# Two transformer blocks on one core: bursts of constant products in TensorE's waits, and ScalarE's untaken path written as loops

## The reference

```
first block, per layer l:
  mod = silu(c) @ w_ada[l] + b_ada[l]            # shifts, scales, gains
  h = norm(x) * (1 + sc1) + sh1
  mix = attention(h)                             # global GQA + three dilated groups, gates
  x = norm(a * x + g1 * mix);  h = norm(x) * (1 + sc2) + sh2
  scores = sigmoid(h @ w_router)                 # 16 experts in 4 groups
  best group, then 2 experts of it; y = sum of silu(h @ gate) * (h @ up) @ down
  x = norm(a * x + g2 * y)
second block: layer 0 gated linear attention, layer 1 differential attention with a relative bias,
  each with an MoE of 16 experts (hidden width 512, in the first block 256), 2 of a group chosen
```

## Time and profile before

| | us |
|---|---|
| median of 3 runs | 1534.39 (1533.79 to 1534.82) |
| the profiled execution's own time | 1536.67 |
| its span, first to last instruction | 1534.9 |
| mean granted TensorE clock | 0.970 |
| busy: PE / DVE / ACT / POOL | 1426.8 (93%) / 546.7 (36%) / 329.3 (21%) / 147.6 (10%) |
| chain that ended last | PE 83%, DMA 7%, DVE 5%, ACT 2%, issue 1% |
| HBM read | 458.24 MB, 301 GB/s over the span |

### The profile page before, as it was taken

One profiled execution on the slowest core, in us unless ns is written; L12 is line 12 of the kernel. 1 busy time (PEld: TensorE's weight loads), 2 busy tenths in 40 slices (PEclk: granted clock), 3 DMA queues, 4 the chain that ended last, 5 costly groups with the idle time before them and its releaser, 6 DMA issues.

```text
span 1534.9 us, 15763 instructions
## 1 busy us (share of the span) xinstructions
PE 1426.8 (93%) x6564; PEld 810.7 (53%) x6564; DVE 546.7 (36%) x1065; ACT 329.3 (21%) x716; POOL 147.6 (10%) x103
## 2 busy tenths in 40 slices
PE   6999999799799999889989998999988998999995
PEld 3686885344378788444336444444435764444432
DVE  2591245532575124553251233121114353322113
ACT  3112231321210323131123132111112343111101
POOL 1007820000002920000000000000000000000000
PEclk8999999899999999989999999999998999999998
DMA  9996352899657741389946557899999408799995
GB/s 376 412 374 241 143 220 110 329 428 418 277 237 287 271 165 56 140 359 429 418 186 244 195 237 311 340 427 429 426 428 400 165 1 338 288 428 427 428 429 236
DMA packets 36873, 462.52 MB, mean 301 GB/s; under 512 B 4120, under 2 KB 6440, under 8 KB 8216
## 3 DMA queue, kind: packets, MB, share of 16 engines
q1 hardware_dynamic: 34112, 448.91, 71.2%
q0 software_dynamic: 1648, 10.39, 1.7%
q10 hardware_dynamic: 1032, 2.10, 0.7%
HBM read 458.24 MB, written 3.15 MB: 301 GB/s over the span
## 4 chain that ended last, share of the span: by engine, by line
PE 83%; DMA 7%; DVE 5%; ACT 2%; issue 1%; SPq 0%; DVEq 0%
PE work L684 12%; PE work L1072 12%; PE acc L684 7%; PE work L667 7%; DMA ring<-in_stream 7%; PE work L957 7%; PE work L1118 6%; PE acc L667 5%; PE work L972 3%; PE acc L817 3%; PE work L676 3%; PE work L1026 2%; PE work L1538 2%; PE acc L1683 2%; PE work L883 2%
## 5 line engine op out<-in xcount | busy, mean ns | idle before, releaser
L684 PE MATMUL work<-ht_sb,ring 128*128 128x256 f32 x576 | 128.0, 383 | 2.1 <-DMA ring<-in_stream 1.6
L684 PEld LDWEIGHTS work<-ht_sb,ring 128*128 128x128 f32 x576 | 110.2, 192 | 19.9 <-DMA ring<-in_stream 2.4
L684 PE MATMUL acc<-ht_sb,ring 128*128 128x256 f32 x512 | 114.0, 381 | 0.0
L1072 PE MATMUL work<-ring,area 128*64 128x512 f32 x480 | 107.9, 593 | 3.4 <-DMA ring<-in_stream 3.4
L684 PEld LDWEIGHTS acc<-ht_sb,ring 128*128 128x128 f32 x512 | 96.1, 190 | 14.8 <-issue 2.0
L667 PE MATMUL work<-ring,ht_sb 128*128 128x512 f32 (+1 forms) x224 | 92.6, 573 | 5.1 <-DMA ring<-in_stream 2.9
L1840 ACT ACTIVATE area<-work 128x512 f32<-128x512 f32 (+1 forms) x53 | 30.6, 590 | 238.8 <-PE work L684 120.7
L2910 DVE SCALAR_TENSOR_TENSOR area<-area,comb_slot,work 128x512 f32<-128x512 f32 x16 | 12.0, 748 | 190.8 <-ACT area L2037 190.8
L535 POOL DMA_DIRECT2D ln_sb<-in_ln_vecs x8 | 4.4, 556 | 778.2 <-DMA early<-in_stream 443.9
L817 PE MATMUL acc<-area_r,mt_sb_r 128*128 128x512 f32 x256 | 71.7, 409 | 5.2 <-DVE area_r L2818 4.3
L667 PE MATMUL acc<-ring,mt_sb 128*128 128x512 f32 x160 | 71.4, 595 | 2.6 <-DVE mt_sb L3138 2.6
(11 more groups left out here) (394 smaller groups left out, 2081.6 us busy)
## 6 DMA issues: line engine op xcount, KB each, us to landing
ring<-in_stream SPq DMA_DIRECT2D x136, 2048.0 KB, 14.8
area<-in_stream SPq DMA_DIRECT2D x46, 2048.0 KB, 15.5
cst<-in_stream SPq DMA_DIRECT2D x14, 2048.0 KB, 14.9
early<-in_stream SPq DMA_DIRECT2D x14, 2048.0 KB, 21.4
ln_sb<-in_ln_vecs POOLq DMA_DIRECT2D x8, 1024.0 KB, 12.2
rel_rows<-mt_sb ACTq DMA_DIRECT2D x1, 2048.0 KB
area<-in_stream SPq DMA_DIRECT2D x2, 1024.0 KB, 10.0
mt_sb<-in_stream SPq DMA_DIRECT2D x2, 1024.0 KB, 16.2
```

What stands on the lines that cost most here:

```text
L684: ins = pe.matmul(dst, w[:, k, c0:c0 + n], src[:, k0 + k, :], start=k == 0, stop=k == ks - 1)
L1072: ins = pe.matmul(banks[half][e * CAP:(e + 1) * CAP, :], tokens[:, k, at:at + CAP], w[:, e, half * W:(half + 1) * W], start=k == 0, stop=k ...
```

## The change

TensorE gets `stay_warm(n)`: n products of a tile of ones with one column of it, spread to 512 columns, in bf16, into a bank that is free there; nobody reads them. Bursts of it are put ahead of and between waits; some of these waits are new and ask for something earlier than the wait that was there. ScalarE's general path becomes three nested loops with two steps written out, so that a loop body has 18 transfers (`moe`).

```diff
+            def stay_warm(n, bank=work[0]):
+                for _ in range(n):
+                    pe.matmul(bank[:, :], ones_h[:, :], ones_h[:, 0:1].to_broadcast([P, W]), start=True, stop=True)
...
             def route_logits(n, ready, between=None):
+                stay_warm(2 if between is None else 5)
                 flip_rows(1, 1, ready)
+                stay_warm(3)
                 route_part(1)
                 fold_part(n, 1)
                 if between is not None:
                     between()
 
+            def await_choice(number):
+                if number < DEPTH:
+                    stay_warm(4)
+                    pe.wait_ge(tokens_scaled, TT * (number + 1))
+                    stay_warm(3)
+                    pe.wait_ge(scores_made, number + 1)
+                    stay_warm(9)
+                    pe.wait_ge(x_hi_ready, TT * (number + 1))
+                    stay_warm(2)
+                else:
+                    stay_warm(2)
+                    pe.wait_ge(logits_made, number + 1)
+                    stay_warm(10)
+                pe.wait_ge(chosen_ready, C.seen(chosen_ready))
+                pe.wait_ge(tables_loaded, 16 * 3)
...
-            def counts():
-                pe.wait_ge(chosen_ready, C.seen(chosen_ready))
-                pe.wait_ge(tables_loaded, 16 * 3)
-                pe.wait_ge(consts_set, 3)
+            def counts(number):
+                await_choice(number)
...
                 pe.matmul(work[1][:, 0:NE], ones_h[:, :], CHOSEN[:, 1, :], start=False, stop=True).then_inc(counted, 1)
+                stay_warm(4)
...
             ada_finish(*ADA_FIRST[3], parts_3)
+            pe.wait_ge(consts_set, 3)
+            stay_warm(4)
+            for k in range(2):
+                pe.wait_ge(ht_by_act, k + 1)
+                stay_warm(3)
             for l in range(DEPTH):
                 if l:
                     spread_silu()
+                    stay_warm(4)
+                    pe.wait_ge(silu_row_ready, 4)
+                    stay_warm(10)
+                    pe.wait_ge(var_ready, 9)
+                    stay_warm(3)
                     flip_tokens(0)
+                    stay_warm(3)
                     await_tokens()
                     wait_acc_free()
-                    pe.wait_ge(silu_row_ready, 4)
...
                       start=True, stop=True).then_inc(filled, 1)
+            stay_warm(3, work[1])
+            pe.wait_ge(var_ready, 17)
+            stay_warm(5, work[1])
             flip_tokens(0)
...
             moe(2, F_2 // P)
+            stay_warm(6)
+            pe.wait_ge(var_ready, 23)
+            stay_warm(5)
             flip_tokens(0)
...
-                with act.Fori(0, PAIRS) as i:
-                    for step in range(steps):
-                        e, f = step // fc, step % fc
-                        act.wait_ge(rest["steps_done"], i * steps + (TT + PAIRS + step))
+                with act.Fori(0, PAIRS) as i, act.Fori(0, 2) as e, act.Fori(0, fc // 2) as d:
+                    for h in range(2):
+                        act.wait_ge(rest["steps_done"], i * steps + e * fc + d * 2 + (TT + PAIRS + h))
                         for q in range(fc):
...
-                                act.dma_start(dst[:, q * ks:(q + 1) * ks, :], w[:, :, o:o + P]).then_inc(rest["loaded"], 16)
+                                act.dma_start(dst[:, q * ks:(q + 1) * ks, :], w[:, :, bass.ds(o, P)]).then_inc(rest["loaded"], 16)
```

More of the change, by code:

```diff
@@ L863, in moe_narrow @@
                 s0, before_pairs = SLOTS[MOE_NAMES[number]], PAIRS * number
-                counts()
+                counts(number)
                 pe.wait_ge(late_drained, len(ADA_LATE) * (number + 1))
@@ L2010, in all_tokens @@
                             for half, dst in enumerate((ALL_GATE, ALL_UP)):
-                                o = (2 * e + half) * fc * P + f * P
-                                act.dma_start(dst[:, q * ks:(q + 1) * ks, :], w[:, :, o:o + P]).then_inc(rest["loaded"], 16)
[L2013 to L2016, removed]
+                                o = e * (2 * fc * P) + d * (2 * P) + (half * fc + h) * P
+                                act.dma_start(dst[:, q * ks:(q + 1) * ks, :], w[:, :, bass.ds(o, P)]).then_inc(rest["loaded"], 16)
+                        w = stream[bass.ds(i * per_pair + d + (s0 + fc), 1), :, :].rearrange("a p n -> p (a n)")
+                        act.dma_start(ALL_DOWN, w[:, bass.ds(e * D + h * 2 * D, D)]).then_inc(rest["loaded"], 16)
+                        act.wait_ge(rest["summed"], i * steps + e * fc + d * 2 + (h + 1))
                         act.activation(ALL_SILU, work[0][:, 0:T], ACT.Silu).then_inc(rest["silu"], 1)
```

## The result

The changed kernel takes 1521.25 us, median of 5 runs (1520.36 to 1521.64), the kernel before 1534.82 (1533.79 to 1536.89, 5 runs): ratio 0.9904, 95% interval 0.9893 to 0.9915. That is 13.6 us won by the medians and 14.7 by the ratio (13.0 to 16.4 by its interval), where 15.3 were forecast (1519.1; the median lies 2.1 above, inside the range).

The account below looks back on a forecast made before the run. TensorE was taken to bound the kernel, with seven stretches at the lower clock behind its waits. Terms of 16.2 us less 0.9 for overruns and gaps gave 15.3, so 1534.4 - 15.3 = 1519.1 us; range 1513 to 1529 (8 in 10).

Parts of the forecast that it names:

- The bound: Whole kernel: TensorE sets the pace (chain 83% PE, 7% DMA), so time won on it is carried to the end.
- bound by DMA: Rival, 5%: the MoEs wait for weight transfers anyway, so their 7.1 us of gain vanish: 1526.2 us.
- First block's gathers: Behind the choice of experts in the first block's two MoEs: a warm clock halves cold gathers, worth 2.29 and 2.84 us.
- The product's price: One burst product of 512 columns: 0.22 us warm, 0.44 cold, taken from a gather's; bounds 0.1 and 0.44.
- Second block's gathers: Behind the choice in the second block's two MoEs: 1.0 us each of 1.7, limited by low parts and ScalarE's copies.
- Norms: Projections behind three layer norms (418.81, 792.74, 1160.57): no longer cold, worth 1.45, 2.23 and 2.64 us.
- ScalarE's delay: Norm behind the third MoE: looping the jumped-over path removes the table load's delay, 2.8 us; rival that it stays, 10%.
- The rule on transposes: Within a 16% rival: flips don't engage the high clock, so projections at 792.74 and 1160.57 lose 4.9 us: 1524.0.
- First loads: Products behind the first modulation rows: worth 0, since time won only lengthens the wait for a weight block at 68.78.
- The eight terms: Four for gathers, three for norms, one for ScalarE: 2.29 + 2.84 + 1.0 + 1.0 + 1.45 + 2.23 + 2.64 + 2.8 = 16.2 us.
- the second fall of the clock in the first layer: Behind the weight-block wait at 68.78: left as it is, with no gain counted for it.

Follow-up runs that it names:

- part 6: Changed kernel with ScalarE's inner loop over d written out, so 36 transfers stand in the wide path instead of 18: 1527.6 us, one run.
- part 5: Changed kernel without the ten products behind the first loads (1520.71 us), or with bursts at two more waits (1519.23, 1520.68); its table counts clock falls in fourteen traces.

## Why the prediction was right, and where not

- **The bound.** Right: the lead grew where TensorE's clock or ScalarE's wait changed, and it was carried to the end through every MoE. The doubled bursts show the same for lost time. Of the rival "bound by DMA" nothing was seen.
- **First block's gathers.** 2.29 + 2.84 forecast, 2.1 + 2.7 in the traces. The bursts fit as reckoned: the choice comes no later (10.36 us behind the flips in the trace after, 10.35 before). The product's price, 0.22 taken from the gathers for want of a row, is what the doubled burst measures.
- **Second block's gathers.** 1.0 each forecast, 0.8 and 0.9 measured. The low parts and ScalarE's copies do hold part of it back.
- **Norms.** 1.45, 2.23 and 2.64 forecast; 1.45, 2.2 and 2.6. The wait of the projections for VectorE's x_sb grew from 0.53 to 1.39 us behind faster flips, as said.
- **ScalarE's delay.** 2.8 forecast; 2.9 in the trace, 3.2 (1.8 to 4.8 by the interval) with the loops alone. That 18 transfers would be short enough was right; that length alone decides isn't borne out (part 6).
- **The rule on transposes** (the Trainium skill, TensorE: Matmul & The Clock Gate, Part 4: PE-mode transpose), by which 1524.0 would have come: not seen in the changed kernel. Between 1145.21 and 1147.70 only flips run, and the projection behind them starts at 1.00, as do the two at 414.36 and 785.72. With the halved bursts the clock holds across the flips behind the third MoE, but falls right behind those of the second block's norm (flips at 786.41, 0.51 from 789 on), so in that kernel the rule isn't excluded.
- **First loads.** Worth nothing, as the run without them shows, but the reason given was wrong. The wait for the weight block became shorter (1.60 to 1.04 us) where it was to become longer, and the burst overran the value it waits for by over 1 us, more than the 0.3 that the prediction allowed. It cost nothing because the warm projection made up for it.
- **Where it missed.** By little, and not clear of noise: 15.3 were forecast, and the ratio's interval reaches from 13.0 to 16.4. The eight terms measure 15.6 us together in the traces (forecast 16.2), where the medians leave 13.6. The step that doesn't hold is the one behind the sum, that the rest of the kernel is alike in both. The prediction left the second fall of the clock in the first layer "as it is", and took from one profile of before which places are cold. Behind waits of 1 to 2 us (68, 150 and 521 us) the clock falls in some executions and not in others. In the two profiled executions this gave 1.7 and took 1.6. By the table of part 5 it takes more from the changed kernel than from the one before: 9 of 12 against 1 of 12, at 1.7 us each in two places, is an estimated 2.3 us, about what the medians lack. That these falls are the missing 2 us is argued, not shown, since the executions behind the medians have no trace.

## What to carry to other kernels

Look for stretches in which TensorE is busy at the lower clock behind a wait of its own, fill the wait with wide products of constants into a free bank up to the moment the awaited value comes, and count one such product as long as a real one of the same columns (0.22 us): an overrun of the wait is passed on to the end like a gain. Fill the wait nearly to its end and take away other engines' delays in it first, since with 2.9 us left empty behind the burst the clock fell again, and 1.6 of the burst's 2.6 us were lost. Code that is never taken can cost time by being jumped over, so if the profile shows an idle time with "issue" as its cause behind the jump, try that path as a loop. A fall of the clock that one profile shows behind a short wait needs several profiles before it is priced.

## What was not expected of the hardware

- The clock's fall behind short waits is not the same from execution to execution: behind the same 1.91 us wait for ScalarE the attention products ran at 1.00 in the first layer, and in the second the clock fell to 0.50 under them (1.09 and 1.69 us for eight).
- A jump over 36 written-out transfers delays the next instruction as long as one over 72 behind the third MoE (5.34 and 5.12 us) and not at all behind the fourth, where 72 cost 1.84 us. One over 20 or 18 costs nothing wherever it stands.
- Halving the bursts lets the clock fall in five places of seven, yet only the two at the norms cost time (1.2 and 1.7 us): a fall that ends before the next real work is free.
